# A final norm made chunk by chunk beside the output product, and a new order of a delta-rule stage's first head

## What is computed

```python
x1 = rms_norm(h, norm_f)                          # end of the first network
hn = rmsnorm(x1, norm_mix_g)                      # start of the second
qkv, gate, a_raw, b_raw = split(hn @ w_in)        # gated delta rule, 8 heads of 128
qkv = silu(causal_dwconv(qkv, conv_w))            # 4 taps
q, k = l2norm(q) * 128 ** -0.5, l2norm(k)
g = -exp(a_log) * softplus(a_raw + dt_bias); beta = sigmoid(b_raw)
# per chunk: G = cumsum(g), tri = I + strict(beta * k k^T * decay), a triangular solve,
# then a state carried over the chunks; norm, gate, output product
h = x1 + mixer; h = h + mlp(rmsnorm(h)); out = rmsnorm(h, final_norm_g)
```

## Time and profile before

| | us |
|---|---|
| median of 3 runs | 3259.73 (3259.64 to 3261.99) |
| the profiled execution's own time | 3261.41 |
| its span, first to last instruction | 3259.7 |
| TensorE matmuls busy | 3143.3 (96%) |
| VectorE busy | 1689.1 (52%) |
| ScalarE busy | 1047.2 (32%) |
| GpSimd busy | 554.2 (17%) |
| mean granted TensorE clock | 0.985 of full |

### The profile page before, as it was taken

One profiled execution on the slowest core, in us unless ns is written; L12 is line 12 of the kernel. 1 busy time (PEld: TensorE's weight loads), 2 busy tenths in 40 slices (PEclk: granted clock), 3 DMA queues, 4 the chain that ended last, 5 costly groups with the idle time before them and its releaser, 6 DMA issues.

```text
span 3259.7 us, 41125 instructions
## 1 busy us (share of the span) xinstructions
PE 3143.3 (96%) x14850; PEld 2545.2 (78%) x14850; DVE 1689.1 (52%) x1929; ACT 1047.2 (32%) x1363; POOL 554.2 (17%) x1011
## 2 busy tenths in 40 slices
PE   6999999999999999998995999999999999999998
PEld 4888888878888888876864788888887788888886
DVE  4546454557767767775224455555555424233333
ACT  3112121245545545543142344444433111111112
POOL 0000000024434434441001222222212000000001
PEclk9999999999999999998997999999999999999999
DMA  3111111131111111115203111111121111111111
GB/s 85 52 46 45 51 46 45 46 97 33 51 30 47 45 32 51 45 43 176 65 20 85 37 36 36 36 39 38 36 73 52 46 46 46 52 45 48 45 49 65
DMA packets 291806, 168.00 MB, mean 52 GB/s; under 512 B 79368, under 2 KB 282120, under 8 KB 291472
## 3 DMA queue, kind: packets, MB, share of 16 engines
q1 hardware_dynamic: 291728, 166.93, 17.9%
HBM read 144.85 MB, written 22.05 MB: 51 GB/s over the span
## 4 chain that ended last, share of the span: by engine, by line
PE 92%; DVE 3%; issue 1%; ACT 1%; SPq 1%; POOL 1%; DMA 0%; DVEq 0%; POOLq 0%; ACTq 0%
PE banks L719 16%; PE banks L721 15%; PE banks L720 15%; PE banks L804 9%; PE banks L806 9%; PE banks L805 9%; PE banks L834 2%; PE banks L1031 1%; PE banks L949 1%; PE banks L1024 1%; PE banks L847 1%; PE banks L849 1%; PE banks L848 1%; PE banks L826 1%; PE banks L825 1%
## 5 line engine op out<-in xcount | busy, mean ns | idle before, releaser
L804 PE MATMUL banks<-state_a_hi,weights_hi 128*128 128x512 f32 x1352 | 579.6, 429 | 21.3 <-DVE conv_in L1813 12.8
L805 PE MATMUL banks<-state_a_lo,weights_hi 128*128 128x512 f32 x1352 | 536.6, 397 | 0.0
L806 PE MATMUL banks<-state_a_hi,weights_lo 128*128 128x512 f32 x1352 | 536.4, 397 | 0.0
L719 PE MATMUL banks<-state_a_hi,weights_hi 128*128 128x512 f32 x1208 | 479.2, 397 | 1.5 <-DVE stream_again L1883 1.5
L721 PE MATMUL banks<-state_a_hi,weights_lo 128*128 128x512 f32 x1208 | 478.1, 396 | 0.0
L720 PE MATMUL banks<-state_a_lo,weights_hi 128*128 128x512 f32 x1208 | 478.1, 396 | 0.0
L1157 ACT ACTIVATE weights_hi<-weights_raw 128x1024 fp32r<-128x1024 f32 x226 | 237.9, 1053 | 658.8 <-PE banks L721 588.3
L1520 DVE TENSOR_TENSOR weights_lo<-weights_raw,weights_hi 128x1024 fp32r<-128x1024 f32 x226 | 298.8, 1322 | 142.3 <-ACT weights_hi L1157 140.4
L804 PEld LDWEIGHTS banks<-state_a_hi,weights_hi 128*128 128x128 f32 x1352 | 257.9, 191 | 65.0 <-DVE weights_lo L1520 14.7
L806 PEld LDWEIGHTS banks<-state_a_hi,weights_lo 128*128 128x128 f32 x1352 | 256.0, 189 | 60.9
L805 PEld LDWEIGHTS banks<-state_a_lo,weights_hi 128*128 128x128 f32 x1352 | 258.1, 191 | 39.1 <-issue 2.1
(11 more groups left out here) (296 smaller groups left out, 4751.9 us busy)
## 6 DMA issues: line engine op xcount, KB each, us to landing
weights_raw<-in_mlp_w_dram SPq DMA_DIRECT2D x64, 512.0 KB, 3.8
weights_raw<-in_gdn_w_in_dram SPq DMA_DIRECT2D x33, 512.0 KB, 4.1
weights_raw<-in_pool_w_in_dram SPq DMA_DIRECT2D x32, 512.0 KB, 3.9
weights_raw<-in_sb_w_in_dram SPq DMA_DIRECT2D x32, 512.0 KB, 4.1
weights_raw<-in_pool_w_out_dram SPq DMA_DIRECT2D x16, 512.0 KB, 3.3
weights_raw<-in_sb_w_in_dram SPq DMA_DIRECT2D x32, 256.0 KB, 4.5
mixed_dram<-stick_gate SPq DMA_DIRECT2D x16, 512.0 KB, 3.3
weights_raw<-in_sb_w_out_dram SPq DMA_DIRECT2D x16, 512.0 KB, 4.9
```

The lines of the kernel that those rows point to most:

```text
L719: pe.matmul(psum[:, bank, :], whi, hi, start=(k == 0), stop=False)
L804: pe.matmul(psum[:, bank, :], whi, hi, start=(k == 0), stop=False)
L805: pe.matmul(psum[:, bank, :], whi, lo, start=False, stop=False)
L806: last = pe.matmul(psum[:, bank, :], wlo, hi, start=False, stop=(k == end - 1))
```

## The change

1. Second group of the output product: behind each tile, ScalarE makes the chunk's scaled copy and both squares, VectorE its rest, GpSimd adds the squares up (chunks 1 to 6). TensorE goes from the last tile directly into the alpha/beta tile and has eight mean products between its halves, in place of 32 behind the product.
2. The second norm's root comes first; the first one's root is kept in `v_by_token`, and the rescaling of the stream is cut in two: chunks 0 and 1 in the log decay chain, 2 to 7 behind the next projection. The store of the stream goes behind the placed blocks of the first head, and what waits for it (the first write to `delta_mixed`) waits at the end of each head.
3. Conv taps, output gain, head parameters, the last-row matrix and the level masks get a place that no earlier stage uses; their loads go between the weight loads of the last pooling group, the masks to GpSimd's start.
4. The first head: matmuls of the next tiles are put between its small products, the k chain goes ahead of the q projection's use, q's taps are spread over waits.

Cut to its core (the line numbers are those of the old and the new file):

```diff
@@ -170,6 +169,8 @@
+        at[0] = max(at[0], free0 + 28 * S * 4)
+        lmask = place("level_masks", [P, LEVELS - LEVEL0, P // 2])
         conv_w = place("conv_taps", [P, TAPS, 3 * HEADS])
@@ -316,14 +319,32 @@
+            def load_group(g, last=False):
                 for c in range(4):
                     load(w_in0[:, :, bass.ds(g * 512 + c * P, P)], KC)
                     load(w_in0[:, :, bass.ds(g * 512 + DI + c * P, P)], KC)
+                    if last and c:
+                        delta_const(c - 1)
...
                 for m in range(4):
                     load(w_out0[:, bass.ds(g * 4, 4), m * 256:m * 256 + 256], 4)
+                    if last:
+                        delta_const(3 + m)
@@ -419,16 +440,6 @@
-            sp.wait_ge(stream_done, 4)
-            sp.dma_start(stream_dram, hacc_o[:, :, :]).then_inc(stream_saved, 16)
-            sp.wait_ge(delta_room, 1)
...
-            for tap in range(TAPS):
-                vec2(conv_w[:, tap, :], t["gdn_conv_w_2"][0, tap].rearrange("(k p) -> p k", p=P))
...
@@ -461,6 +472,8 @@
             place_blocks()
+            sp.wait_ge(rescaled, KC)
+            sp.dma_start(stream_dram, hacc_o[:, :, :]).then_inc(stream_saved, 16)
@@ -606,26 +634,19 @@
+            for c in range(1, KC - 1):
+                for w in range(2):
+                    pool.wait_ge(mid_squared, 2 * c + w + 1)
+                    if c > 1:
+                        pool.wait_ge(mid_summed, 2 * c + w - 3)
+                    pool.tensor_tensor(y_stage[w][:, :], y_stage[w][:, :], squares_o[w][:, :], ALU.add).then_inc(mid_summed, 1)
             pool.wait_ge(delta_room, 1)
...
@@ -910,17 +920,22 @@
-            norm_both(squares_o)
-
-            pe.wait_ge(state_lo, st_lo.add(KC))
...
+            base = [tile.fixed]
+            for k in range(KC):
+                pe.wait_ge(state_lo, st_lo.add())
+                gemm_part(base[0], 0, k, k + 1, A)
+            for w in range(2):
+                for part, x in enumerate((y_stage, squares_o)):
+                    pe.wait_ge(*((mid_squared, 2 * KC - 1 + w) if part else (mid_summed, 2 * (KC - 2) - 1 + w)))
+                    for h in range(2):
+                        last = pe.matmul(psum[:, 4 + 2 * w + h, :], mean_of[:, :], x[w][:, h * HALF:(h + 1) * HALF], start=(part == 0), stop=(part == 1))
+                last.then_inc(mid_mean, 1)
+            gemm_part(base[0], 1, 0, KC, A)
             ring_tile()
-            pe.wait_ge(pre_pool, PRE_POOL)
-            for part in range(2):
-                ring_tile()
...
@@ -1081,14 +1100,20 @@
-            for h in range(2):
-                scores_k(h)
-            ring_tile()
+            base[0] = tile.fixed
+            gemm_part(base[0], 0, 0, 4, A)
+            scores_k(0)
+            gemm_part(base[0], 0, 4, 6, A)
+            scores_k(1)
+            gemm_part(base[0], 0, 6, KC, A)
+            gemm_part(base[0], 1, 0, KC, A)
...
+            gemm_part(base[0], 0, 0, KC, A)
             turn_k()
             scores()
-            ring_tile()
+            gemm_part(base[0], 1, 0, KC, A)
@@ -1313,21 +1320,31 @@
-            finish_both()
-
+            for c in range(KC):
+                split_weights(halves.value())
+                halves.add(2)
+                act.wait_ge(mid_chunk, c + 1)
+                act.activation(A_hi[:, c, :], hacc_o[:, c, :], ACT.Copy, scale=gains[:, 3, c:c + 1]).then_inc(state_hi, 1)
+                for w in range(2):
+                    if c >= 2:
+                        act.wait_ge(mid_summed, 2 * c - 3 + w)
+                    act.activation((squares_o if c else y_stage)[w][:, :], hacc_o[:, c, :], ACT.Square,
+                                   scale=gains[:, 2, c:c + 1] if w else 1.0).then_inc(mid_squared, 1)
             act.preload_act_table_set(LN_EXP)
+            split_weights(halves.value())
...
+            act.wait_ge(mid_means_joined, 1)
+            root(inv[:, :], inv[:, :], 1)
+            root(vn[:, :, :].rearrange("p c n -> p (c n)"), two_banks(4), 0)
@@ -1745,37 +1764,31 @@
+            for c in range(KC):
+                split_weights()
+                for h in range(2):
+                    src = take()
+                    dst = hacc_o[:, c, h * HALF:h * HALF + HALF]
+                    dve.tensor_tensor(dst, dst, src, ALU.add).then_inc(bank_free, 1)
+                dve.wait_ge(bank_free, half.value(4))
+                dve.sem_inc(mid_chunk, 1)
                 dve.wait_ge(state_hi, sth.add())
...
@@ -1799,9 +1816,14 @@
             did("cl", dve.tensor_scalar(sp8[:, :], gT8[:, :], 40.0, None, ALU.min))
+            dve.wait_ge(norm_act, nact.add(2))
...
+            rescale(0, 2)
             dve.wait_ge(pre_act, PRA["ln"])
@@ -1975,15 +1999,21 @@
             normed_k()
+            tap(qT, 2, slice(0, 1))
             system(0)
             system(1)
+            tap(qT, 3, slice(0, 1))
+            split_weights()
+            dve.wait_ge(conv_done, 2)
             for h in range(2):
                 evac(h)
+            rescale(2, KC)
             normed_q()
```

More of the change, by code:

```diff
@@ L326, in _ @@
                     load(w_out0[:, bass.ds(g * 4, 4), m * 256:m * 256 + 256], 4)
+                    if last:
+                        delta_const(3 + m)
+            with turns(sp, GROUPS - 1, [(tile, 14)]) as g:
+                load_group(g)
+            load_group(GROUPS - 1, True)
             QK, V0 = SB_HEADS * SB_QK, 2 * SB_HEADS * SB_QK
@@ L729, in norm @@
                     last.then_inc(norm_pe, 1)
-            def norm_both(squares):
-                for k in range(KC):
-                    for w, bank in enumerate((5, 3)):
-                        pe.wait_ge(square_done, sq.add())
-                        if w == k == 0:
-                            pe.wait_ge(bank_free, half.value(4))
-                        for h in range(2):
-                            last = pe.matmul(psum[:, bank + h, :], mean_of[:, :], squares[w][:, h * HALF:(h + 1) * HALF], start=(k == 0), stop=(k == KC - 1))
-                        last.then_inc(norm_pe, 1)
             pe.wait_ge(consts_made, N_CONSTS)
@@ L1747, in _ @@
             ysh, back = Tally(KC), [Tally(), Tally()]
-            for grp in range(2):
-                with turns(dve, 4, [(tile, 2), (half, 4)] + [(ysh, 2), (back[0], 16), (back[1], 16)] * (grp == 0)) as i:
-                    for m in range(2):
-                        split_weights()
-                        if grp == 0:
-                            dve.wait_ge(y_split_hi, ysh.add())
-                            one = lambda x: x[:, bass.ds(2 * i + m, 1), :].rearrange("p a n -> p (a n)")
-                            dve.tensor_tensor(one(B_lo), y_stage[m][:, :], one(B_hi).bitcast(F32), ALU.subtract).then_inc(y_split_lo, 1)
-                            dve.wait_ge(stream_back[m], back[m].add(16))
-                        for h in range(2):
-                            src = take()
-                            dst = hacc_o[:, bass.ds(2 * i + m, 1), h * HALF:h * HALF + HALF].rearrange("p a n -> p (a n)")
-                            dve.tensor_tensor(dst, dst, src, ALU.add).then_inc(bank_free, 1)
@@ L1778, in _ @@
+            dve.sem_inc(stream_done, 2)
             dve.sem_inc(delta_room, 1)
+            split_weights()
             pre = [0]
@@ L1839, in _ @@
             did("bn", dve.tensor_copy(bn[:, :, :], pg(6)))
+            for i in range(TAPS):
+                tap(kT, i, slice(HEADS, HEADS + 1))
+            split_weights()
+            dve.wait_ge(conv_done, 1)
+            evac(0)
             dve.wait_ge(pre_pe, 2)
@@ L1846, in _ @@
             after("neg")
+            evac(1)
+            for i in range(2):
+                tap(qT, i, slice(0, 1))
             ev = Events(dve, "dve")
```

171 lines of the change are left out of this document (84 added, 87 removed).

## The result

The changed kernel takes 3204.36 us (median of four, 3203.35 to 3207.83), the one before 3260.86 (median of four, 3259.64 to 3267.1): a ratio of 0.9825, 95% interval 0.9808 to 0.9842, 56.5 us less. The forecast was 3200.0, 59.8 less. TensorE is busy for 3113.7 us of it, 97%.

A forecast was written before the change was run, and what follows sets the result against it. TensorE, busy for 96%, was taken as the bound, with its idle time sought in the 151 us before the first head. A gain of 62.0 less 2.2 given back made 59.8 us, so 3200 us, range 3190 to 3212.

The forecast's parts named there:

- Norm by chunks: Output product: each chunk's norm work fits beside its 11.2 us turn and costs nothing, with 4.4 us to spare.
- rival 3: Output product: GpSimd's additions hold up VectorE's split and stretch the turns, giving 3214 to 3228 us; chance 0.05.
- TensorE's row: From product to k sums: TensorE runs 41.7 us of work without waits, so the k sums start at 1717.5.
- Both margins under 2 us: Alpha/beta scaling ready at 1692.1, wanted at 1693.9; log decays ready at 1703.2, wanted at 1705.1.
- Inversion: GpSimd block inversion before the first head: VectorE's twelve instructions hold up its steps, so it takes 22.7 us.
- Transfers: The system's way through DRAM to the inversion and back before the first head: stays at 14.4 us.
- The restart: First head's start: after nearly 15 us idle, TensorE runs at half clock and gives back 2.2 us.
- Store and constants: The stream's store behind the placed blocks, and constants loaded in the last pooling group, each cost nothing.
- The signs that it named: Profile marks to confirm or refute it, among them 11.2 us turns, first product near 1765, first head not over 83 us.
- Rival 1: Inversion held up no more than before: 3195.4 us, or 3191 with nothing held up; chance 0.2.
- rival 2: The k path loses its small margins or the store delays the second decay row: 3204 to 3212 us; chance 0.16.
- the slower case: Output product turns grow to 20 us, making the kernel slower than before, 3270 us; chance 0.01.

The follow-up runs named there:

- e1: Changed kernel with the six rescales during the block inversion reading their second operand from PSUM: 3200.21 us.
- e2: Changed kernel with the six rescales moved behind the block inversion: 3199.48 us.
- e8: Changed kernel with two rescales before the inversion, and four rescales, v's taps and the last take behind it: 3197.17 us.
- e10: Same kernel as e8, run five times beside the changed kernel: median 3197.2 us.
- e4: Changed kernel without the store of the rescaled stream: 3203.53 us.
- e6: Changed kernel with the seven loads of constants issued behind the output product instead of in the last pooling group: 3203.91 us.
- e5: Kernel before with only the constants and masks moved to their own place, constants loaded in the last pooling group, masks made at GpSimd's start: 3246.5 us.
- e11: The changed kernel itself, unaltered, run five times again: median 3204.02 us.
- e7: Changed kernel with the norm's ScalarE, VectorE and GpSimd work put behind the output product again, TensorE's order kept: 3229.64 us.
- e3: Changed kernel with 56 matmuls of no use in TensorE's idle time before the first head: 3203.96 us.
- e9: e8 with 31 matmuls of no use filling TensorE's wait before the first head: median of five 3196.25 us.

## Why the prediction came out right, point by point

- **Norm by chunks: right.** The turns stay at 11.2 us (second halves taken at 1597.46 and 1608.66), TensorE is busy for all 90 us of eight turns. GpSimd's pair of additions took 5.90 instead of the 4.8 of the forecast, and the split 1.70 from the second turn on, as rival 3 feared, but it ends at 1615.3 and TensorE wants that tile at about 1620. The longer split took half a microsecond of the cover.
- **TensorE's row: right.** Mean products in 6.87 (forecast 7.1), no gap over 1 us, log decays at 1702.9 (1703.2), k sums from 1717.1 (1717.5), first k logarithm at 1718.2 (about 1718), the system's end at 1727.4 (1727.7). Both margins under 2 us held. What the forecast did not have is that GpSimd also holds VectorE up (last section): it stretched k's taps by 1.5, a split by 0.9 and q's first tap by 1.9. The taps of k and the split fitted under TensorE's tiles. The first tap of q stands in the chain of waits, but ScalarE's last instruction for k's norm ends at 1721.85 and VectorE goes on with it at 1721.97, so the tap cost 0.1 at most.
- **Inversion: right in kind, 0.8 too short.** Twelve steps held up under the run of twelve, one under the q decay: 23.5 us to the end of the last instruction, as the forecast counts, against 22.7. One of the twelve, the first of the four taps, has a single tensor operand, which the forecast did not tell apart; its step took 0.61. The page "SBUF — State Buffer" of the Trainium skill (section "Who interferes with whom") says that a VectorE instruction with two SBUF inputs contends with a GpSimd instruction that reads SBUF, and one with at most one such input, outside the two-port modes, does not. By that rule the two kernels e1 and e2 had to come out as they did, and the trace agrees.
- **Transfers: right**, 14.5 against 14.4. The first product came at 1765.46, forecast 1764.8: 61.3 us gained up to there instead of 62.0. That is 0.3 early from the k path, 0.8 late from the inversion and 0.1 from the transfers.
- **The restart: the term that was mis-sized.** "So 2.2 us go back": it was 3.3, 28.0 us to the next exponential against 24.7. The estimate took its price from twelve wide matmuls, 5.3 us long; here the clock came back only 7 us after the first product, and in that time lay the sixteen thin products (1.7 more), the eight transposes (0.9 more) and about six wide matmuls. It also took off 0.3 that the kernel before would pay already; the trace before shows nothing paid (24.70 us, clock 1.00). The size is not a fixed one: the clock came back 5.4 us after the first product in e8 and 8.5 in e10, the same kernel, and the exponential came 27.3 and 28.7 behind it. So 2.6 to 4.0 us is what the runs show for this wait and a wait of 7.2 alike, and 2.2 lies under all of it. From this exponential on the second head stands 58.0 us earlier (1851.49 to 1793.48), and at the next one still (1931.33 to 1873.29).
- **Store and constants: right.** The store costs nothing (e4), and neither do the constants in their new place (e6 has them elsewhere and takes the same stage time, 172.7). The taps took 0.57 us to issue in the pooling stage, not the 2.3 forecast. The removal of the constants alone gains 15 (e5), not the 20 that its row in the chain suggests, since the store is late next.
- **1.2 us that no term has.** 58.0 are gained at the second head, 56.8 at the end. 0.5 goes in the MLP, 0.7 in the last additions and the output, where neither the code nor the order changed. The second profile of the changed kernel (e11) does not show either: from the norm behind the delta stage to the first addition of squares of the last norm it takes 682.7 us, as the kernel before (683.2 in the first profile), and from there to the output's first transfer 88.7 (before 88.6, first profile 89.3). So this is scatter between executions, not a cost of the change. In e11 other scatter makes up for it: its delta stage starts 1.3 later, and its span is 3203.2.
- **The signs that it named.** All came but one. "If the first head lasts over 83 us" was to mean wrong, and it lasts 83.2 (1765.46 to 1848.66; 79.9 before). It is the same 3.3 of the restart once more. And where it named a dozen slow matmuls behind the wait there are nearly thirty, most of them thin.

So the sum was 59.8, and it came to 62.0 - 0.7 - 3.3 - 1.2 = 56.8. The misses of the three parts all have the same sign, so none hid another. Rival 1 fell with the twelve long steps, rival 2 with the row without gaps and with e4, rival 3 with the turns of 11.2, and so did the slower case. The median of 3204.36 lies 0.4 above the forecast case's 3197 to 3204, where the forecast had priced rival 2, but what put it there is the restart and not rival 2's lost margins or a late row.

Some sums in the forecast are off by a little, and none moves it by more than 0.2: 1675.98 and 41.7 make 1717.7 and not 1717.5, thirty steps of 0.44 and 0.6 make 13.8 and not 13.9. Of its prices for unlikely cases, the one where only the 20 us of constants go should be about 3240 and not 3235, and turns of 20 us give about 3260 and not 3270.

## What to carry to other kernels

When a long helper chain on GpSimd sets the end, look at what VectorE does beside it: an instruction of 1.3 us with two SBUF operands costs it about 0.8 us, one whose second operand is in PSUM nothing, and moving ten instructions (six rescales, four taps) out of the chain's time made it 8 us shorter here, and the kernel 7, with no work removed. Before you pay for moving small transfers, see what stands in front of them in their queue: seven constants were worth 15 us behind a 4 MB store and nothing without it. And price a wait of TensorE by how long the clock stays at half behind it, as a range: here the clock stayed at half for 5.4 to 8.5 us of work behind waits of 7.2 to 14.4, and 2.6 to 4.0 us were lost.

## What the runs showed that I had not expected

**VectorE is held up too.** What the forecast calls a lock works both ways: where GpSimd starts first, it is VectorE's instruction that gets longer. From the timelines of VectorE and GpSimd in the changed kernel:

```profile
1706.77 5.45 DVE L1844 SCALAR_TENSOR_TENSOR k_conv<-conv_in,conv_taps,k_conv 128x1024 f32<-128x1024 f32 x3
1712.13 2.10 DVE L1539 TENSOR_TENSOR weights_lo<-weights_raw,weights_hi 128x1024 fp32r<-128x1024 f32 x1
...
1718.10 2.63 DVE L1841 TENSOR_SCALAR q_or_v_conv<-conv_in,conv_taps 128x1024 f32<-128x1024 f32 x1
```

```profile
1709.23 1.90 POOL L657 TENSOR_TENSOR decay_matrix<-log_decay_row,log_decay_by_token 128x1024 f32<-128x1024 f32 x1 [19.90 <-DMA log_decay_row<-log_decay_dram]
1711.36 1.80 POOL L661 TENSOR_SCALAR_AFFINE_SELECT decay_matrix<-decay_matrix 128x1024 f32<-128x1024 f32 x1 [0.23 <-POOL decay_matrix L657]
1717.40 1.90 POOL L665 TENSOR_TENSOR decay_times_beta<-decay_matrix,beta_by_token 128x1024 f32<-128x1024 f32 x1 [4.24 <-ACT decay_matrix L1365]
```

Three taps took 5.45 instead of 3.93, a split 2.10 instead of 1.22, and a product of one SBUF tensor and a scalar, 0.75 elsewhere, took 2.63 under GpSimd's 1.90. So an operation with a single tensor operand can be blocked too. The same section of the Trainium skill names `tensor_scalar` among the operations that can take both ports, and says that the order of issue decides who waits; these rows agree. The forecast had no such term. It cost next to nothing here, because TensorE's tiles and ScalarE's part of k's norm took as long.

**A gain of a few microseconds may not reach the end.** The last head starts with waits of its own, and the clock falls there in some executions for longer than in others. Between the first and the last request of the stream's return (two marks that the same work separates) lie 75.9 us in the changed kernel (2337.45 to 2413.34), 75.8 in the kernel before, 74.0 in e2 and e10, 73.3 in e7, 75.8 in e8 and e3, 78.1 in e9 (2328.56 to 2406.69). e9 entered it 3.6 us before e10 and left it 0.6 after it. The tables of stretches, e9 and then e10:

```profile
2320.00:2360.00 40.00, 34.83 (x184) 31.53 (x183) 17.35 (x24) 17.01 (x17) 0.00 (x0) 0.74 0.36 105
```

```profile
2320.00:2360.00 40.00, 34.83 (x209) 31.41 (x208) 19.44 (x25) 18.82 (x19) 0.00 (x0) 0.87 0.38 115
```

Busy for the same 34.83 us, with 184 matmuls at a clock of 0.74 in the one and 209 at 0.87 in the other. This is where the gain of e9's profiled execution went; the other four have no trace. What decides which of them an execution gets was not tried.
